# One layer of a hybrid SSD, attention and retrieval trunk: the score matmuls of a round of four heads issued in six groups inside the gate unit beside them

## The reference

```python
scores = jnp.einsum('bqhd,bkhd->bhqk', q_blk, k).astype(jnp.float32) * scale
mask = key_chunk[None, :] <= q_chunk[:, None]
probs = jax.nn.softmax(jnp.where(mask, scores, -jnp.inf), axis=-1).astype(v.dtype)
return jnp.einsum('bhqk,bkhd->bqhd', probs, v)
...
g = jax.nn.sigmoid((g_logits + b_gate)...)
mix = jnp.dot(g[:, :, 0] * y_ssd + g[:, :, 1] * y_mla, w_mix_out)
```

## Time and profile before

| | us |
|---|---|
| median of 3 runs | 3150.56 (3145.92 to 3153.97) |
| span of the profiled execution | 3150.4 |
| attention stage (four rounds) | about 215 to 500 |
| PE busy over the span | 1502.7 (48%) |
| DVE busy over the span | 2491.9 (79%) |

### The profile page before, as it was taken

One profiled execution on the slowest core, in us unless ns is written; L12 is line 12 of the kernel. 1 busy time (PEld: TensorE's weight loads), 2 busy tenths in 40 slices (PEclk: granted clock), 3 DMA queues, 4 the chain that ended last, 5 costly groups with the idle time before them and its releaser, 6 DMA issues.

```text
span 3150.4 us, 30493 instructions
## 1 busy us (share of the span) xinstructions
PE 1502.7 (48%) x10239; PEld 1364.1 (43%) x10239; DVE 2491.9 (79%) x2630; ACT 686.9 (22%) x702; POOL 697.9 (22%) x728
## 2 busy tenths in 40 slices
PE   1299999899999999998949000000000000000000
PEld 1288888888888889998749000000000000000000
DVE  7855547788888785444555999999999999999999
ACT  1143334244444444433323000000000000000000
POOL 0000001122222230000011333333332333333332
PEclk8598889999999999999979555555555555555555
DMA  7845556866656665656524999999998899999997
GB/s 267 308 139 164 173 174 228 274 211 207 214 190 201 201 201 174 232 183 213 183 85 165 381 388 388 385 415 385 385 376 358 342 388 369 402 389 373 385 384 294
DMA packets 255647, 880.10 MB, mean 279 GB/s; under 512 B 19496, under 2 KB 56976, under 8 KB 188208
## 3 DMA queue, kind: packets, MB, share of 16 engines
q0 software_dynamic: 93600, 614.51, 49.1%
q1 hardware_dynamic: 161872, 264.11, 25.4%
q10 hardware_dynamic: 64, 0.07, 0.0%
HBM read 876.49 MB, written 2.13 MB: 279 GB/s over the span
## 4 chain that ended last, share of the span: by engine, by line
DVE 51%; PE 37%; issue 7%; ACT 3%; DMA 1%; SPq 0%; DVEq 0%; POOL 0%; ACTq 0%
DVE ps L1809 18%; DVE rrow L1791 17%; PE ps L601 9%; PE ps L602 8%; PE ps L603 8%; DVE acc L1302 4%; DVE wlo L1240 2%; ACT whi L917 2%; PE ps L581 2%; PE ps L582 1%; PE ps L583 1%; PE aux L799 1%; PE aux L750 1%; PE aux L748 1%; PE aux L747 1%
## 5 line engine op out<-in xcount | busy, mean ns | idle before, releaser
L1240 DVE TENSOR_TENSOR wlo<-raw,whi 128x2048 fp32r<-128x2048 f32 x216 | 515.8, 2388 | 413.0 <-ACT whi L917 396.4
L1809 DVE SCALAR_TENSOR_TENSOR ps<-rrow,wgt,ps 128x2048 f32<-128x2048 f32 x256 | 603.1, 2356 | 12.4
L917 ACT ACTIVATE whi<-raw 128x2048 fp32r<-128x2048 f32 x216 | 413.2, 1913 | 821.0 <-PE ps L603 493.0
L1791 DVE CUSTOM_DVE_ANT_0 rrow<-rrow,aux 128x2048 f32<-128x2048 f32 x256 | 566.5, 2281 | 7.3 <-issue 6.7
L601 PE MATMUL ps<-h_hi,whi 128*128 128x256 f32 (+1 forms) x1568 | 458.6, 292 | 14.4 <-DVE wlo L1240 6.8
L602 PE MATMUL ps<-h_lo,whi 128*128 128x256 f32 (+1 forms) x1568 | 448.5, 286 | 0.0
L603 PE MATMUL ps<-h_hi,wlo 128*128 128x256 f32 (+1 forms) x1568 | 448.4, 286 | 0.0
L1937 POOL DMA_INDIRECT rrow<-in_peer_v,eid x256 | 239.8, 937 | 542.7 <-DVE ps L1809 380.2
L1937 POOL DMA_INDIRECT rrow<-in_peer_u,eid x256 | 241.0, 941 | 468.7 <-DVE dots L1791 186.8
L601 PEld LDWEIGHTS ps<-h_hi,whi 128*128 128x128 f32 (+1 forms) x1568 | 304.4, 194 | 30.3 <-issue 15.8
L1302 DVE SCALAR_TENSOR_TENSOR acc<-ada_in,csil,acc 128x512 f32<-128x512 f32 x360 | 295.6, 821 | 25.8 <-DMA ada_in<-in_w_ada 4.4
(11 more groups left out here) (299 smaller groups left out, 2752.7 us busy)
## 6 DMA issues: line engine op xcount, KB each, us to landing
raw<-in_w_in SPq DMA_DIRECT2D x120, 1024.0 KB, 5.2
ada_in<-in_w_ada POOLq DMA_DIRECT2D x128, 512.0 KB, 5.0
ada_in<-in_w_ada SPq DMA_DIRECT2D x32, 1024.0 KB, 5.2
raw<-in_w_ssd_out SPq DMA_DIRECT2D x32, 1024.0 KB, 5.1
raw<-in_w_mla_out SPq DMA_DIRECT2D x16, 1024.0 KB, 7.3
raw<-in_w_mix_out SPq DMA_DIRECT2D x16, 1024.0 KB, 5.1
raw<-in_peer_w_q SPq DMA_DIRECT2D x16, 1024.0 KB, 5.0
raw<-in_w_ukv SPq DMA_DIRECT2D x8, 1024.0 KB, 5.4
```

Source lines behind the costliest of these rows:

```text
L917: F(whi[:, n % 2, :, 0:cols_], raw[:, n % 4, :, 0:cols_], ACT.Copy).then_inc(hi_ready, 1)
L1240: V.tensor_tensor(wlo[:, n % 2, :, 0:cols_], raw[:, n % 4, :, 0:cols_], whi[:, n % 2, :, 0:cols_].bitcast(F32), ALU.subtract).then_inc(lo_ ...
L1791: last = V.tensor_tensor_reduce(row, row, auxf, 1.0, 0.0, ALU.mult, ALU.add, dots[:, k, e:e + 1])
L1809: V.scalar_tensor_tensor(psf, row, wgt[:, k, e:e + 1], psf, ALU.mult, ALU.add)\
```

## The change

`channel_unit` gets an argument `between`, a function called after the three matmuls of each tile, except the last. For unit 4 it issues groups of scores after every second tile from the second `kc` on; the last score is issued behind the unit. The three waits move in front of the first group. Every matmul stays what it was; nothing changes on the other engines.

```diff
-            def channel_unit(base, j, i, per, x_hi, x_lo, k0, klast, tiles, kcs=4, used=True, width=P):
+            def channel_unit(base, j, i, per, x_hi, x_lo, k0, klast, tiles, kcs=4, used=True, width=P, between=None):
...
                         last = mm(o, wl, x_hi[:, k, :], start=False, stop=(k == klast), skip_group_check=True)
+                        if between is not None and not (kc == kcs - 1 and t == len(tiles) - 1):
+                            between(kc, t)
...
-                    channel_unit(U_ATT, 4, i, N_ATT, h_hi, h_lo, 0, DC - 1, slab_tiles(0))
-
-                    pe.wait_ge(att_evac_a, i + 1)
-                    pe.wait_ge(att_evac_v, i + 1)
-                    pe.wait_ge(qpe_read, i + 1)
-
-                    for h in range(4):
...
-                        for b in range(BLK):
...
-                    last.then_inc(scores_done, 1)
+                    def scores_between(kc, t):
+
+                        if kc == 0 or t % 2 == 0:
+                            return
+                        if (kc, t) == (1, 1):
+
+                            pe.wait_ge(att_evac_a, i + 1)
+                            pe.wait_ge(att_evac_v, i + 1)
+                            pe.wait_ge(qpe_read, i + 1)
+                        step = 2 * (kc - 1) + t // 2
+                        if step == 0:
+                            score(0, 0)
+                            score(1, 0)
+                        elif step == 3:
+                            score(2, 0)
+                            score(3, 0)
+                        elif step in (1, 2):
+                            score(step - 1, 1)
+                        else:
+                            score(2, 1)
+
+                    channel_unit(U_ATT, 4, i, N_ATT, h_hi, h_lo, 0, DC - 1, slab_tiles(0), between=scores_between)
+                    score(3, 1).then_inc(scores_done, 1)
```

More of the change, by code:

```diff
@@ L598, in channel_unit @@
                     k = k0 + kc
-                    for o, c, first in tiles:
+                    for t, (o, c, first) in enumerate(tiles):
                         wh, wl = hi[:, kc, c:c + width], lo[:, kc, c:c + width]
@@ L734, in _ @@
                     last.then_inc(qpe_turned, 1)
-                    channel_unit(U_ATT, 4, i, N_ATT, h_hi, h_lo, 0, DC - 1, slab_tiles(0))
-                    pe.wait_ge(att_evac_a, i + 1)
-                    pe.wait_ge(att_evac_v, i + 1)
-                    pe.wait_ge(qpe_read, i + 1)
-                    for h in range(4):
-                        r = slice(64 * (h % 2), 64 * (h % 2) + 64)
-                        for b in range(BLK):
[L744 to L751, removed]
@@ L752, in _, with score @@
-                    last.then_inc(scores_done, 1)
+                    def score(h, b):
+                        r = slice(64 * (h % 2), 64 * (h % 2) + 64)
+                        nk = P * (b + 1)
+                        o = aux[:, h, b * P:b * P + nk]
+                        t = slice(b * P, b * P + P)
+                        mm(o, qn[:, h, t], kn[:, h, 0:nk], start=True, stop=False)
+                        mm(o, qpeT[r, h // 2, t], kpeT[r, 0:nk], start=False, stop=False)
+                        return mm(o, con[0:1, C_MQ:C_MQ + P], con[0:1, C_MK + 256 - nk:C_MK + 256],
+                                  start=False, stop=True)
```

## The result

The changed kernel takes 3189.64 us (median of 4 runs, 3167.82 to 3192.67), the kernel before 3149.5 in the same comparison: ratio 1.0109, 95% interval 1.0089 to 1.013. The forecast was 3187 us, 3158 to 3197, slower. One of the four runs, with 3167.82 us, stands well apart from the other three (3189.37 to 3192.67).

The account below looks back on a forecast made before the run. PE's stream bounds the attention stage, at half clock among unit 4's scores. A round: 5.3 us until the waits end, plus 28.8 at half, less 0.5: 33.6 against 24.36. Four rounds add 37 to 3150.4: 3187 us, range 3158 to 3197.

Parts of the forecast that it names:

- clock down as soon as the waits end: Bound for unit 4 of each attention round: half clock right after the waits, +9.7 us a round (+39).
- The sum for a round: Unit 4's first matmul to unit 5's: 5.3 us, then 28.8 at half clock, less 0.5; 33.6 us against 24.36.
- The switches: PE changing between gate and score matmuls in unit 4: taken at nothing, bound 1 us a round, at most 4 in all.
- Everything behind it unchanged: Sign in the profile after: attention stage longer by 37 us, everything behind the stage unchanged in length.
- No recovery within the mix: Unit 4: once down, the clock stays at half among scores and gate matmuls, 28.8 us for 30 gate matmuls and all scores.
- the rival with a chance of 0.13: Unit 4: clock lost at the waits but back among the mixed matmuls; 3160 us, between 3148 and 3172; chance 0.13.
- the thin rows: Attention scores: matmuls using 128, 64 and 1 rows, not PE idleness, drop the clock; mean 0.72 from unit 4 to 5.
- the gate matmuls do not keep the scores warm: Unit 4: 1.3 us of gate between score groups cannot restore the clock, where 3.95 to 5.94 us uncut were needed.
- What hid: Behind unit 4's scores: maxima start about 1.2 us late; 8.7 us to ready probabilities stays hidden under 11.5 us of PE work.
- The clock that is kept: Rival: gate matmuls hold full clock through unit 4's scores; -5.1 us a round, -20 us, 3130 us; chance 0.11.
- The wait behind the maxima: Rival: probabilities over 2.8 us later than worked out make PE wait ahead of L758; 3191 us for one microsecond; chance 0.02.

## Why the prediction was right

**The wait.** Foretold: 3.0 us four times for DVE's copy `vt`, PE arriving at about 237.8. Measured: four times 3.0, 12.0 us, with PE there at 237.46. In the run where only the wait moved it costs 17 us, half clock included.

**The fall of the clock.** Foretold: 5 to 8 us after the unit's start. In round 1 it came at 7.0 us, with 1.6 us of scores at full clock where I had taken 0.7. In rounds 2 to 4 it came at the end of the wait, just before the scores began, and these rounds are the longer ones by 1.2 us: that is the bound "clock down as soon as the waits end". The first score pairs of round 2:

```profile
321.02:323.00 1.98, 1.98 (x6) 1.46 (x6) 1.79 (x3) 0.00 (x0) 0.20 (x1) 0.50 0.59 198
```

The sum for a round was 33.6 us, measured 33.90; four rounds make 38 us where 37 were foretold. The switches, taken at nothing, came to nothing at half clock as well: the first gate matmul of a group takes 0.38 us instead of 0.21 (243.53 to 243.91), and the first score pair behind gate 0.98 instead of 1.15 (244.98 to 245.96). "Everything behind it unchanged" missed by 2.6 us. The median, 3189.64 us, lies 2.6 us above the forecast; the stage of the profile grew by 37.5 us.

**No recovery within the mix.** That was the step with the least in the trace before to stand on. It holds for the four rounds of the first profile, and by their times for seven of nine runs. Two runs had the recovery, one of them in rounds 2 and 4 by its profile. So the rival with a chance of 0.13 is real, its price (each further microsecond at half costs 0.44) is right, and the reason why the clock comes back in some rounds and not in others is open.

**What makes the clock fall.** The prediction blamed the thin rows. The mask with 128 rows bears this out for the block (same order, same count, no fall), with the reserve that its pairs also came closer together. The mix without the wait shows that gate matmuls between do hold the clock up when it is up at the start: all four rounds at 1.00. I had written that the gate matmuls do not keep the scores warm, which held only behind the gap; that sentence was wrong as a general one, but the sum did not hang on it. Gap and scores each have a share. In the changed kernel the clock was down before the first score in three rounds and 1.6 us after it in one; where only the wait moved, it was down at the end of the gap in two rounds and stayed up in the other two until the scores. So the gap alone can bring it down but does not always, and the prediction did not weigh the two.

**What hid.** DVE's rest of unit 6 now ends just ahead of the maxima, in the changed kernel's DVE timeline of round 1 (against the earlier trace rows):

```profile
266.95 2.29 DVE L1239 TENSOR_TENSOR wlo<-raw,whi 128x2048 fp32r<-128x2048 f32 x1 [23.72 <-ACT whi L916]
269.16 1.82 DVE L1488 TENSOR_REDUCE st<-aux 128x4 f32<-128x512 f32 x2
...
274.82 1.83 DVE L1496 TENSOR_TENSOR probs<-probs,st 128x512 f32<-128x512 f32 x2
```

The maxima start 269.16 - 268.05 = 1.1 us behind the scores (1.2 foretold), and the probabilities are ready at 276.65, 5.1 us before PE needs them at 281.76.

**Busy and the clock.** PE is busy without a break from unit 4 to unit 5 with a mask of 1 row and with one of 128, at a mean clock of 0.71 in the one and 1.00 in the other. The Trainium skill, "TensorE: Matmul & The Clock Gate", section "Part 1: The HAM clock gate (the "warmup" mystery)", ties the clock to how busy the PE has been. These runs show that the busy time of a profile is not enough to tell the clock by.

**Against the rivals.** The clock that is kept did not come about in any profiled round of the change. It is what the run without the wait shows, 3122.79 us; the forecast for that case was 3130 with the wait's 12 us in it, so 3118 without. The wait behind the maxima did not come about either.

## What to carry to other kernels

Before mixing thin matmuls into a dense stream, look up in the profile when the operands of the first of them are ready, not those of the last: a group that starts before they are ready makes PE wait, and everything queued behind it. Read the granted clock beside the busy time; here a PE that was 100% busy ran at half clock while a third of its score matmuls had a single row, and filling the rows with zeros was a cheaper cure than another order. The new order cost 39 us, the same order without the gap gained 28, and full rows in the old order gained 51.

## What the hardware showed that I had not expected

An fp32 matmul with few rows was not cheaper here than one with 128, but dearer, at the same clock, and it made its neighbours dearer. In a block of scores with 128, 64 and 1 rows the pairs take 0.42 us (128 columns) and 0.63 (256). With 128 rows in all of them they take 0.22 and 0.43, 0.2 us less a pair. With only the mask at 128 rows some are 0.31 to 0.33 and 0.53. It looks as if the next weights are loaded under a running matmul only when both matmuls have the full 128 rows. The records of the weight loads (PEld) fit this. L747's load behind the mask, first with the mask at 128 rows and then in the kernel before:

```profile
241.47 0.30 PEld L747 LDWEIGHTS aux<-kn,qn 128*128 128x128 f32 x2
242.56 0.30 PEld L747 LDWEIGHTS aux<-kn,qn 128*128 128x128 f32 x2
```

The first begins 0.11 us ahead of its matmul, which starts at 241.58; the second begins with its matmul, at 242.56. No run here has other mixtures of rows, so the rule itself is not shown. The Trainium skill, "TensorE: Matmul & The Clock Gate", section "Part 3: Packing small matmuls — row/col tiling", says that weight loads overlap with running matmuls only when the row group differs; the same section also lets a load run ahead into a background weight buffer. These fp32 matmuls do not follow the first statement: the overlap is there between matmuls on the same 128 rows and not seen between 128, 64 and 1.

Rows of zeros served as well as rows of data. In the run with the mask at 128 rows, 127 of its rows are zeros, and the clock stayed at 1.00; with zeros in the rotated keys the time is 3100.29 us, with data in their place 3101.22.
